# Recurrence set-up of a fused two-block kernel: input matrices turned a quarter at a time, kernel products placed between them, one exponential moved

## The reference

```python
u = (h @ w_in).reshape(bsz, seq, SSM_GROUPS, SSM_CH)
...
bu_re = jnp.einsum('bsgc,gpc->bsgp', u, bbar_re)
bu_im = jnp.einsum('bsgc,gpc->bsgp', u, bbar_im)
...
_, _, xs_re, xs_im = lax.associative_scan(combine, (a_re, a_im, bu_re, bu_im), axis=1)
y = (jnp.einsum('bsgp,gcp->bsgc', xs_re, c_re)
     - jnp.einsum('bsgp,gcp->bsgc', xs_im, c_im)
     + d_skip[None, None] * u)
z = jax.nn.gelu(y.reshape(bsz, seq, SSM_WIDTH))
z = z * jax.nn.sigmoid(z @ w_glu)
return z @ w_out
```

## Time and profile before

| | |
|---|---|
| time of 3 runs | median 1314.8 us (1314.05 to 1314.8) |
| the profiled execution's own time | 1318.43 us |
| its span, first to last instruction | 1316.6 us |
| PE busy | 1256.2 us, 95% |
| DVE, ACT, POOL busy | 950.8, 672.3, 424.5 us |
| mean granted PE clock | 0.986 |

### The profile page before, as it was taken

The page is one execution under the profiler, slowest core; times in us unless marked ns, Lnnn a source line. Parts: engine busy times, 40 slices in busy tenths (PEclk is TensorE's granted clock), DMA queues, the critical chain, the costliest instruction groups (busy, mean ns, idle before and its releaser), DMA issues.

```text
span 1316.6 us, 21079 instructions
## 1 busy us (share of the span) xinstructions
PE 1256.2 (95%) x7823; PEld 1072.4 (81%) x7850; DVE 950.8 (72%) x1439; ACT 672.3 (51%) x1103; POOL 424.5 (32%) x217
## 2 busy tenths in 40 slices
PE   6999999998889999999999999999999999999998
PEld 5866888876667688888788888798999967899997
DVE  7776777676775665556686755468999875799997
ACT  5565444444455444444464544356556643555553
POOL 3014444544211455554344322100000013344543
PEclk9999999999989999999999999999999999999999
DMA  7045665645212566665366533255445514366663
GB/s 231 16 140 182 187 196 178 199 143 175 81 65 80 163 193 191 188 190 150 114 222 192 160 97 97 65 147 161 150 151 159 160 62 146 104 190 189 191 190 112
DMA packets 168927, 197.61 MB, mean 150 GB/s; under 512 B 12542, under 2 KB 133886, under 8 KB 168830
## 3 DMA queue, kind: packets, MB, share of 16 engines
q1 hardware_dynamic: 167499, 192.01, 47.6%
q10 hardware_dynamic: 1362, 4.74, 1.0%
HBM read 195.14 MB, written 1.05 MB: 149 GB/s over the span
## 4 chain that ended last, share of the span: by engine, by line
PE 74%; DVE 13%; DMA 5%; ACT 5%; issue 2%; POOL 1%; SPq 0%; DVEq 0%; ACTq 0%
PE acc L707 23%; PE wk L659 9%; PE wk L621 7%; PE wk L622 7%; PE wk L623 7%; PE wk L661 5%; DMA raw<-in_w_in 2%; DVE LO L475 2%; PE wk L1193 1%; ACT HI L1438 1%; PE acc L926 1%; PE acc L1219 1%; PE acc L621 1%; PE acc L622 1%; PE acc L623 1%
## 5 line engine op out<-in xcount | busy, mean ns | idle before, releaser
L475 POOL TENSOR_TENSOR LO<-raw,HI 128x1024 fp32r<-128x1024 f32 (+1 forms) x158 | 393.4, 2496 | 568.8 <-ACT HI L1438 500.0
L1438 ACT ACTIVATE HI<-raw 128x1024 fp32r<-128x1024 f32 (+3 forms) x382 | 366.1, 995 | 132.9 <-PE acc L707 38.7
L475 DVE TENSOR_TENSOR LO<-raw,HI 128x1024 fp32r<-128x1024 f32 (+1 forms) x156 | 222.7, 1431 | 84.6 <-ACT HI L1438 84.2
L621 PE MATMUL wk<-X,HI 128*128 128x256 f32 x784 | 225.2, 287 | 4.1 <-ACT arena L1872 1.7
L622 PE MATMUL wk<-X,HI 128*128 128x256 f32 x784 | 222.5, 284 | 0.0
L623 PE MATMUL wk<-X,LO 128*128 128x256 f32 x784 | 222.4, 284 | 0.0
L659 PE MATMUL wk<-X,HI 128*128 128x512 f32 x512 | 183.7, 401 | 2.5 <-DVE X L2024 2.5
L621 PEld LDWEIGHTS wk<-X,HI 128*128 128x128 f32 x784 | 150.8, 192 | 7.9 <-issue 3.3
L622 PEld LDWEIGHTS wk<-X,HI 128*128 128x128 f32 x784 | 150.9, 193 | 1.0
L623 PEld LDWEIGHTS wk<-X,LO 128*128 128x128 f32 x784 | 150.9, 193 | 0.0
L661 PE MATMUL wk<-X,LO 128*128 128x256 f32 x512 | 144.1, 281 | 0.0
(11 more groups left out here) (393 smaller groups left out, 2077.1 us busy)
## 6 DMA issues: line engine op xcount, KB each, us to landing
raw<-in_mlp_w SPq DMA_DIRECT2D x128, 512.0 KB, 4.1
raw<-in_w_in SPq DMA_DIRECT2D x100, 512.0 KB, 4.4
raw<-in_w_up SPq DMA_DIRECT2D x44, 512.0 KB, 4.0
raw<-in_w_down SPq DMA_DIRECT2D x44, 256.0 KB, 3.2
raw<-in_att_w_in SPq DMA_DIRECT2D x16, 512.0 KB, 4.1
raw<-in_w_ssd_proj SPq DMA_DIRECT2D x16, 512.0 KB, 3.6
raw<-in_att_w_out SPq DMA_DIRECT2D x8, 512.0 KB, 3.6
raw<-in_w_out SPq DMA_DIRECT2D x8, 512.0 KB, 4.1
```

What stands on the lines that cost most here:

```text
L475: tensor_tensor(LO[:, s, cs], raw[:, s % 2, "ab".index(part), 0:m], HI[:, s, cs].bitcast(F32), ALU.subtract).then_inc(S(f"lo_{part}"), 1)
L621: mm(o, lh, rh, start=start, stop=False, skip_group_check=skip)
L1438: A(HI[:, s, j * m:(j + 1) * m], raw[:, s % 2, j, 0:m], ACT.Copy).then_inc(S(f"hi_{part}"), 1)
```

## The change

PE: call `g` now turns part `g % 2` of quarter `g // 2`, so that a quarter has both its parts after two calls. All eight calls stand behind the second `w_in` product, where before two stood in its middle. The calls, the first two drives and the four quarters of `kernels5` alternate. `kernels5` has lost its 16 products of zeros. The last two drives follow the skip product, and 18 products of zeros stand in front of `within` instead of 8. In all, the `keep_busy` calls from the first turned input to `within` issue 22 products of zeros where they issued 41.

ACT: the copy for the second half of `u5` goes ahead of the first `inputs_out`; six instead of four of the `inputs_out` copies stand behind the sines of `e5`. The exponential of `alog` moves from ahead of the gelu to behind the gate.

```diff
-                r, q = g // 4, g % 4
+                q, r = g // 2, g % 2
...
-            def kernels5(half):
-
-                for i in range(8 * half, 8 * half + 8):
-                    keep_busy(spare5, 1)
+            def kernels5(q):
+
+                for i in range(4 * q, 4 * q + 4):
                     for r in range(2):
                         mm(accf[:, 1536 + i * 32:1568 + i * 32], w5[:, r, i, :], ct5[:, r, i, :], start=(i == 0 and r == 0),
                            stop=False, skip_group_check=True)
-                if half == 0:
-                    return
+
+            def skip_added():
+
+                pe.wait_ge(S("dd5_ready"), 1)
...
-            used(ch_major(arrived(), 1, between=first_inputs))
-            for g in range(2, 8):
-                keep_busy(spare5, 2)
-                inputs_turned(g)
+            used(ch_major(arrived(), 1))
+            pe.wait_ge(S("ct_ready"), 1)
+            pe.wait_ge(S("cols_ready"), 2)
+            turned_pair(0)
+            kernels5(0)
+            keep_busy(spare5, 2)
+            turned_pair(1)
             pe.wait_ge(S("u5_in0"), 16 * 16)
+            drive(0)
+            kernels5(1)
+            turned_pair(2)
+            pe.wait_ge(S("bt_ready"), 4)
+            drive(1)
+            kernels5(2)
+            turned_pair(3)
+            kernels5(3)
+            skip_added()
+            pe.wait_ge(S("u5_in1"), 16 * 16)
+            pe.wait_ge(S("bt_ready"), 8)
+            drive(2)
             keep_busy(spare5, 2)
-            pe.wait_ge(S("bt_ready"), 8)
-            drive(0)
-            keep_busy(spare5, 1)
-            drive(1)
-            kernels5(0)
-            pe.wait_ge(S("dd5_ready"), 1)
-            kernels5(1)
-            pe.wait_ge(S("u5_in1"), 16 * 16)
-            for q in range(2, 4):
-                keep_busy(spare5, 1)
-                drive(q)
-            keep_busy(spare5, 8)
+            drive(3)
+            keep_busy(spare5, 18)
             pe.wait_ge(S("m5_ready"), 1)
...
-            inputs_out(0, 2)
             to_steps(1)
-            inputs_out(2, 4)
+            inputs_out(0, 2)
...
-            inputs_out(4, 8)
+            inputs_out(2, 8)
...
-            act.wait_ge(S("late_in"), 16 * N_LATE)
-            A(alog[:, :], alog[:, :], ACT.Exp).then_inc(S("alog_ready"), 1)
-
             for first, end in ((0, 2), (2, 3), (3, 4)):
...
                     .then_inc(S("z2_hi"), 1)
+            act.wait_ge(S("late_in"), 16 * N_LATE)
+            A(alog[:, :], alog[:, :], ACT.Exp).then_inc(S("alog_ready"), 1)
             hi_to(6)
```

More of the change, by code:

```diff
@@ L831, in _, with turned_pair @@
             spare5 = accf[:, 1024:1536]
[L833 to L838, removed]
-            used(ch_major(arrived(), 1, between=first_inputs))
-            for g in range(2, 8):
-                keep_busy(spare5, 2)
-                inputs_turned(g)
-            pe.wait_ge(S("u5_in0"), 16 * 16)
-            keep_busy(spare5, 2)
-            pe.wait_ge(S("bt_ready"), 8)
-            drive(0)
-            keep_busy(spare5, 1)
-            drive(1)
-            kernels5(0)
-            pe.wait_ge(S("dd5_ready"), 1)
-            kernels5(1)
-            pe.wait_ge(S("u5_in1"), 16 * 16)
-            for q in range(2, 4):
-                keep_busy(spare5, 1)
-                drive(q)
-            keep_busy(spare5, 8)
+            def turned_pair(q):
+                inputs_turned(2 * q)
+                inputs_turned(2 * q + 1)
+            used(ch_major(arrived(), 1))
[5 more added lines that the diff above has]
+            turned_pair(1)
+            pe.wait_ge(S("u5_in0"), 16 * 16)
+            drive(0)
[10 more added lines that the diff above has]
+            drive(2)
+            keep_busy(spare5, 2)
+            drive(3)
+            keep_busy(spare5, 18)
             pe.wait_ge(S("m5_ready"), 1)
@@ L1542, in inputs_out @@
             def inputs_out(first, end):
-                for r, q in ((g // 4, g % 4) for g in range(first, end)):
-                    act.wait_ge(S("bt_psum"), 4 * r + q + 1)
-                    A(wt5[:, 4 * q:4 * q + 4, r, :], wk[:, 2 + q % 2, :].rearrange("p (a n) -> p a n", a=4), ACT.Copy)\
+                for g in range(first, end):
+                    q, r = g // 2, g % 2
+                    act.wait_ge(S("bt_psum"), g + 1)
+                    A(wt5[:, 4 * q:4 * q + 4, r, :], wk[:, 2 + r, :].rearrange("p (a n) -> p a n", a=4), ACT.Copy)\
                         .then_inc(S("bt_ready"), 1)
@@ L1565, in _ @@
             padded(1)
+            to_steps(1)
             inputs_out(0, 2)
-            to_steps(1)
-            inputs_out(2, 4)
             act.wait_ge(S("angle5_part"), 3)
```

## The result

The changed kernel takes **1327.47 us** (median of 4, 1326.35 to 1329.49) where the kernel before takes 1314.45 (median of 4, 1314.05 to 1314.8). The ratio is 1.0098, 95% interval [1.0082, 1.0114]: slower by 1.0%. I had forecast 1310.0 with a range to 1313.8. The prediction was wrong in its direction.

The account below looks back on a forecast made before the run. PE was taken as the bound: busy 95% of the span, 74% of the last-ending chain. `within` 5.3 us sooner, less 0.5 for the slow profiled execution, gave -4.8 on the 1314.8 median: 1310.0 us, range 1308.5 to 1313.8.

Parts of the forecast that it names:

- the price of PE's narrow products: PE, first turned input to `within`: 1.85 us per quarter of kernel products and 1.89 per drive, without fillers, full clock.
- the third rival: PE's clock stays low from the first drive till the fillers: `within` 5 to 7 us later, 1320 to 1322; chance 0.08.
- it had sped up while only transposes ran: PE's transposes from 11.53 us: 0.20 us each at first, 0.116 later, read as transposes keeping the clock up.
- the rule that the prediction set against the row: The Trainium skill's statement that a PE transpose doesn't count as busy for the clock in the way a product does.
- The counter-argument that failed: Against the clock staying low: PE's drives without fillers, 1.89 us each, ran while the clock rose.
- The first half of `u5`: SP's sixteenth transfer, which the first drive waits for: starts at 40.5, lands 1.8 us later, at 42.3.
- PE's durations at the full clock: PE up to the skip: product ends at about 37.6, a quarter of kernels takes 1.85 us, the skip 0.98.
- The padding is late next: ACT's padding of `cq5` ends at 56.5, behind `kk_psum` at 54.4; ten copies follow, `within` 5.3 us sooner.
- The 18 fillers: PE's products of zeros ahead of `within`: 4.2 us, ending at 62.9, with no slack, so any PE delay shows in full.
- The exponential: ACT: moving it from ahead of the gelu gains at most 0.15 us; at its new place hidden, at most 0.2 lost.
- Passing the shift on to the end: Everything behind `within` hangs on it through waits alone, so its 5.3 us shift reaches the end of the run.

Follow-up runs that it names:

- the exponential back: The changed kernel with the exponential of `alog` back ahead of the gelu: 1325.48 us, ratio 1.0051 against the kernel before.
- eight behind: The changed kernel with 8 instead of 18 products of zeros behind the last drive: 1323.25 us, ratio 1.0047 against the kernel before.
- both edits: The changed kernel with fillers ahead of each tile, nine ahead of the `u5` wait, eight behind the last drive: 1313.3 us, and 1313.92 timed again.

## Why the prediction was wrong

**The step that failed** is the price of PE's narrow products: 1.85 us for each quarter of kernels and 1.89 for each drive, at the full clock throughout, though their fillers had been taken out. The effect of that on the clock entered the sum as nothing. The prediction noted that nowhere in the trace do kernel products run without a filler, but put the question of the clock to the turned pairs alone: "By that rule the turned pairs would count as idle, and the clock would fall among them, which is the third rival below; by the row they hold it." Measured, a quarter of kernels took 3.57 at the lower clock, a drive 3.57, and the stage lost 8.9 us by it (4.5 + 2.8 + 1.6 in the ledger).

This was the third rival, "the clock stays low", which decides "from 10.6 us of low clock on". The two stretches of the profile, 43.6 to 53.8 and 60.7 to 70.9, are 20.4 us together. I gave it 0.08. Its price for the stage, `within` 5 to 7 later, is near the measured 4.9, but by luck: the sum was too low. With the skip at 66.5, two drives, two fillers and 18 fillers at the full clock alone end at 75.0; there was no working for 73, and none for drives and fillers at the lower clock. In the profile the clock came back for 6.9 us in between, while the profiles with a low stretch of 27 us have `within` at 73.95 (with eight fillers) and 76.10. The rival's time of 1320 to 1322 was too low.

The profiled execution of before had itself a low stretch in this place that cost it 68.10 - 66.86 = 1.2, by the profile of the version with only the exponential moved, whose clock is at 1.00 there. So, if the median executions of before had no such stretch, which no profile shows, the stage of this profile accounts for 4.9 + 1.2 = 6.1 of the 13.0 between the medians; the rest stays open (above).

**The reading of the earlier trace rows** that "it had sped up while only transposes ran" doesn't hold. The windows of the kernel before are

```profile
11.50:14.20 2.70, 2.67 (x13) 1.00 1.09 328
14.20:17.60 3.40, 3.40 (x31) 1.00 1.16 334
17.60:21.00 3.40, 3.07 (x14) 0.51 0.98 307
```

The clock was at 1.00 already in the first full transposes, so 0.20 against 0.116 us is not a rise of the clock; and behind 6 us of nothing but transposes it fell, in this profile and in some of the others, though not in all. So the trace did not speak against the rule that the prediction set against the row, and doesn't prove it either. No run here changes the turned pairs alone. They are not needed for the fall, as it comes in the kernel before without tile fillers, 8 us behind the last of them; and they stand in the four profiles of the rearranged kernel with tile fillers, where the clock held through all of them.

**The counter-argument that failed:** "Against: the drives without fillers, 1.89 us each, ran while the clock rose." Of the first two drives before, only the second took 1.89 us, from 49.88 on the earlier trace rows; the first started at 47.35, in the low stretch, and took 2.5. And each drive had a filler or two ahead of it. Without one right ahead, and where the clock was low, drives took 3.57 us in the changed kernel, 3.52 and 3.68 with the exponential back, and 3.51 and 3.68 with eight behind.

**The first half of `u5`:** the sixteenth transfer started at 40.59 (40.5 predicted) and landed 2.85 later, not 1.8. I had used the median of 32 transfers for one of them: 1.1 us mis-sized.

**PE's durations at the full clock were right.** The product ended at 37.50 (37.6), a quarter of kernels takes 1.87 (1.85), from the fourth quarter's start to the skip's end it is 2.8 (2.8).

**"The padding is late next" was right.** In each of the profiles with a full clock the copies of the kernels follow the padding with no wait, and `within` follows the copies. The term was mis-sized: 3.4 sooner where I had 5.3, and 66.86 - 64.71 = 2.2 sooner than the kernel before has it in the profile without its low stretch. In the profile of both edits drive 0 starts at 43.90 where I had 42.3 (+1.6: the transfer, and nine fillers that run a little past it), and the padding at 54.55 where I had 52.2, so another 0.75. Most of that is the tile fillers that the clock needs: a tile with its filler has a period of 0.58 us, a quarter 2.3 where I had 1.85, and two quarters stand between drive 0 and the last pair. From the padding's start to `within` it is 10.2 us, where I had 10.35.

**The 18 fillers.** I called them without slack ("any delay of PE shows in full"), and it showed: ACT was through at 68.14, and PE at 72.99. Whether eight would have been better at that clock was tried and is not settled.

**The exponential:** at its old place it cost some 0.4 to 0.5 us, not at most 0.15; at its new one it is all but hidden, as predicted (its load measured 1.28 and itself 0.23, I had 0.28): POOL's low part of piece 5 starts 98.97 - 79.51 = 19.46 us behind the gelu, where before it was 94.17 - 74.83 = 19.34. No run can tell it in the whole time.

**Passing the shift on to the end** was right to within 2.1 us in ten of the twelve other profiles (the table's last column against 1241.8). For the changed kernel's own profile it was not: 4.2 us came on top.

## What to carry to other kernels

Products of zeros between narrow products are part of the schedule. Before taking one out, ask what the clock does in the rows around it, and price the whole stage behind it at half the clock; the loss is larger than the filler's own time by far. Sixteen fillers of at most 0.24 us each were worth 7 us here (1323.56 against 1316.7). Put back into the rearranged kernel they give ratios of 0.9976 to 0.9986 in its four timings; one interval, with nine more over the wait and the exponential at its old place, lies below 1 (0.9976 [0.9961, 0.9991]), the others reach 1.0002 and 1.0003. Fillers make a fall rarer, and don't rule it out: the kernel before had them in the profile with 30 us of low clock. For a single transfer that ends a wait, take that transfer's own row and not the median of its queue.

## What the hardware showed that I had not expected

- PE can have its queue full and still be given the lower clock. In the kernel before without tile fillers PE was busy 20.07 of 20.40 us at a granted clock of 0.50. The Trainium skill ("TensorE: Matmul & The Clock Gate", Part 1, What's actually happening) says that the gate goes by how busy PE has been; the trace doesn't agree, if busy is what the profile counts as busy. The work in this stretch was in the main f32 products of 32 and 64 columns, each with a full load of weights.
- Such a stretch can last: 27.3 us in one profile, where the one in the first profile of the kernel before was 3.4. It can last through fillers as well: over 30 us in the second profile of the kernel before, with one product of zeros to every two of the kernel's.
- Whether the clock falls differs between executions of one program: the version with the exponential back has two executions at 1313 and eight above 1322. Such a program has two times, and one profile shows one of them; the mean granted clock of each execution tells them apart.
- At the full clock, 16 products of 32 columns (1.87 us) and 16 of 64 columns (1.89) take the same time; at the lower one too (3.57 and 3.57 as listed). Both are paced by something other than their columns. I take it to be the load of weights (listed with means of 191 and 202 ns for the two in the kernel before), which no run varies by itself.
